# Starting the attention head pairs before the low-rank projections are done, and alternating the kinds of pair

## The reference, cut to what matters

```python
a_q, a_k, a_v, b_q, b_k, b_v, c_q, c_kv, c_kr = jnp.split(h @ w_in, IN_OFFSETS, axis=-1)
y_a = _window_attn(q_a, k_a, v_a, k_a_ctx, v_a_ctx, sink_a)      # 4 heads, windowed, with a sink
y_b = _gqa_core(q_b, k_b_all, v_b_all)                           # 4 heads, rms-normed q and k
q = _heads(_rms_norm(c_q, mla_q_norm) @ w_uq, C_HEADS)           # 8 heads, compressed path
k_nope, v = _rms_norm(c_kv, mla_kv_norm) @ w_uk, ... @ w_uv
y = concat(y_a, y_b, y_c) @ w_out
```

## Time and profile before

| what | value |
|---|---|
| median of 3 runs | 1936.54 us (1934.94 to 1938.43) |
| the profiled execution | 1939.29 us, its span 1937.5 us |
| granted clock, mean of the span | 0.953 |
| PE busy | 1744.1 us, 90% |
| DVE busy | 942.6 us, 49% |
| ACT busy | 645.5 us, 33% |
| mix0, from the fifth `uq` to the first `w_out` matmul | 945.47 to 1083.09 us |
| mix1, the same stretch | 1599.25 to 1694.86 us |

### The profile page before, as it was taken

How to read it: one execution, slowest core, us unless ns; L and a number is a source line. 1 busy time by engine, 2 the same in 40 slices (tenths; PEclk the granted TensorE clock), 3 DMA queues, 4 the chain that set the end, 5 groups by cost and what they waited for, 6 DMA issues and landing times.

```text
span 1937.5 us, 22581 instructions
## 1 busy us (share of the span) xinstructions
PE 1744.1 (90%) x9106; PEld 1191.6 (61%) x9106; DVE 942.6 (49%) x1702; ACT 645.5 (33%) x1110; POOL 94.8 (5%) x136
## 2 busy tenths in 40 slices
PE   6988967998998779989989979999999798889998
PEld 5654733444676334447445658888888574578886
DVE  5573410002344000144487465888766756755555
ACT  2155121122232112132266445222222424655443
POOL 0790000000000000000000000000000100000000
PEclk8998989999999889999989989999999898999999
DMA  9977499999857999982200112445544131024540
GB/s 395 377 304 319 173 416 416 421 421 421 364 215 324 409 405 417 422 348 87 87 1 1 44 44 87 180 189 191 200 181 189 38 114 44 1 87 174 176 172 22
DMA packets 62899, 430.04 MB, mean 222 GB/s; under 512 B 6592, under 2 KB 10816, under 8 KB 10944
## 3 DMA queue, kind: packets, MB, share of 16 engines
q1 hardware_dynamic: 62784, 428.48, 55.4%
HBM read 427.40 MB, written 1.05 MB: 221 GB/s over the span
## 4 chain that ended last, share of the span: by engine, by line
PE 64%; DVE 15%; DMA 10%; ACT 7%; issue 2%; SPq 1%; DVEq 0%; ACTq 0%
PE bank L292 14%; PE bank L1100 12%; PE bank L296 8%; PE bank L298 8%; PE bank L297 8%; DMA ring<-in_ws_dram 7%; DMA work<-in_ws_dram 3%; DVE ring_halves L2457 3%; ACT work_halves L2451 2%; PE bank L331 2%; PE bank L2110 1%; PE bank L2087 1%; DVE work L438 1%; PE bank L2555 1%; PE bank L2481 1%
## 5 line engine op out<-in xcount | busy, mean ns | idle before, releaser
L296 PE MATMUL bank<-work_halves 128*128 128x512 f32 (+1 forms) x1088 | 397.7, 366 | 25.8 <-DVE HH_halves L2886 8.5
L298 PE MATMUL bank<-work_halves,ring_halves 128*128 128x512 f32 (+1 forms) x1088 | 388.0, 357 | 0.0
L297 PE MATMUL bank<-HH_halves,work_halves 128*128 128x512 f32 (+1 forms) x832 | 288.6, 347 | 0.0
L1100 PE MATMUL bank<-ring,work 128*32 128x512 f32 (+2 forms) x896 | 258.6, 658 | 20.2 <-DMA work<-in_ws_dram 11.0
L1100 PE MATMUL bank<-work 128*32 128x512 f32 (+2 forms) x640 | 222.7, 650 | 33.9 <-DMA ring<-in_ws_dram 32.0
L296 PEld LDWEIGHTS bank<-work_halves 128*128 128x128 f32 x1088 | 208.7, 192 | 62.7 <-DVE HH_halves L2886 14.0
L298 PEld LDWEIGHTS bank<-work_halves,ring_halves 128*128 128x128 f32 x1088 | 208.5, 192 | 28.8
L2457 DVE TENSOR_TENSOR ring_halves<-ring,work_halves 128x2048 fp32r<-128x2048 f32 x72 | 163.6, 2288 | 51.0 <-ACT work_halves L2451 51.0
L297 PEld LDWEIGHTS bank<-HH_halves,work_halves 128*128 128x128 f32 x832 | 160.7, 193 | 20.7 <-issue 2.2
L1378 DVE TENSOR_TENSOR work<-work,bank 128x512 f32<-128x512 f32 x14 | 9.6, 688 | 296.7 <-PE bank L1100 296.7
L2451 ACT ACTIVATE work_halves<-ring 128x2048 fp32r<-128x2048 f32 x72 | 136.0, 1906 | 29.7 <-PE bank L298 28.0
(11 more groups left out here) (367 smaller groups left out, 2523.4 us busy)
## 6 DMA issues: line engine op xcount, KB each, us to landing
ring<-in_ws_dram SPq DMA_DIRECT2D x287, 1024.0 KB, 10.2
work<-in_ws_dram SPq DMA_DIRECT2D x117, 1024.0 KB, 17.9
con<-in_con_dram SPq DMA_DIRECT2D x1, 1177.0 KB, 27.5
XX<-in_xT_dram SPq DMA_DIRECT2D x1, 1024.0 KB, 10.2
XX<-in_cT_dram SPq DMA_DIRECT2D x1, 1024.0 KB, 21.3
out_dram<-XX SPq DMA_DIRECT2D x1, 512.0 KB, 3.6
out_dram<-XX SPq DMA_DIRECT2D x2, 256.0 KB, 2.8
par<-in_par_dram SPq DMA_DIRECT2D x1, 338.0 KB, 3.1
```

Of the source, the lines that this page charges most:

```text
L296: pe.matmul(out, l[0], r[0], start=start, stop=False)
L297: pe.matmul(out, l[0], r[1], start=False, stop=False)
L298: return pe.matmul(out, l[1], r[0], start=False, stop=stop)
L1100: m = pe.matmul(b[c, :], left[:, k, c], ring_of(self.w[i])[:, 512 * k:512 * k + 512], start=first and k == 0, stop=last and k == 3, skip_g ...
```

## The change

The late steps are taken out of the first part but for `uq` 0 to 3. Their order becomes uq 4, uq 5, rot 0, uq 6, uq 7, rot 2, uk 0, uk 1, rot 4, uk 2, uk 3, rot 6, uk 4 to 7, uv 0 to 3, and they are dealt out over the first eight pairs, up to three to a pair (`share`), one behind each of PE's three pieces of work in an iteration. They use banks 6 and 7 in turn; meanwhile scores have 0, 1, 2 and results only 5. ACT and DVE get the matching copies: the first of an iteration ahead of ACT's part of `act_rest` and the exponentials (on DVE behind the maxima), the others at the iteration's end.

The pairs are listed by hand. In mix0 the first eight are the A and B pairs of the context queries, alternating (256 keys); then four times A 512, C 512, C 256 and four times B 512, C 512, C 256. In mix1 the first eight are A and B in turn, then the eight C.

The two splits of `w_out` move to iterations 19 and 21 (mix0) and 9 and 11 (mix1) on ACT, at the end of the iteration, and to the head of the next iteration on DVE. The score buffers `sc` now lie where the first split writes. After the square root for `kB`, ACT does one small Exp into an unused column.

```diff
-                for h in range(8):
+                for h in range(4):
                     ro.take("uq", h)
                     self.events.append(("uq", h))
...
+                rest = [("uq", 4), ("uq", 5), ("rot", 0), ("uq", 6), ("uq", 7), ("rot", 2), ("uk", 0), ("uk", 1), ("rot", 4), ("uk", 2), ("uk", 3), ("rot", 6)]
+                rest += [("uk", h) for h in range(4, 8)] + [("uv", i) for i in range(4)]
+                if self.last:
+                    pairs = [(0, 0), (0, 2), (0, 1), (0, 3), (1, 0), (1, 2), (1, 1), (1, 3)] + [(q, c) for q in range(2) for c in range(4, 8)]
+                    share = [3, 3, 3, 3, 2, 2, 2, 2]
+                else:
+                    pairs = [(2, 0), (2, 2), (2, 1), (2, 3), (3, 0), (3, 2), (3, 1), (3, 3)]
+                    share = [3, 3, 3, 3, 3, 3, 2, 0]
+                    for a in range(2):
+                        for i in range(4):
+                            pairs += [(i // 2, 2 * a + i % 2), (i // 2, 4 + 2 * a + i % 2), (2 + i // 2, 4 + 2 * a + i % 2)]
...
+                self.spare = len(share) + 1 if self.last else 19
...
+                    for u in self.pair(i):
+                        put(0, (0, 1, 2) if both else (0, 1, 2, 7), "s", u)
...
+                        for ev in self.between[i][j:j + 1]:
+                            put(3, (6, 7), *ev)
...
                 for i in range(len(self.units) // 2 + 2):
                     for u in self.pair(i):
                         self.pe_scores(pe, u)
+                    for ev in self.between[i][0:1]:
+                        self.pe_late(pe, ev)
                     for u in self.pair(i - 1):
                         self.pe_turn(pe, u)
+                    for ev in self.between[i][1:2]:
+                        self.pe_late(pe, ev)
                     if i >= 2:
                         self.pe_values(pe, 2 * i - 4)
+                    for ev in self.between[i][2:3]:
+                        self.pe_late(pe, ev)
...
+                        if name == "kB":
+                            act.activation(small[:, 250:251], ones[:, 0:1], ACT.Exp)
...
                 for i in range(len(self.units) // 2 + 1):
-                    if i in (3, 5):
-                        self.ffn.split_act(act, i // 4)
+                    for ev in self.between[i][0:1]:
+                        self.act_late(act, ev)
...
+                    for ev in self.between[i][1:3]:
+                        self.act_late(act, ev)
+                    if i == self.spare:
+                        st.wait_ge(act, "qrope", 6)
+                        self.ffn.split_act(act, 0)
+                    if i == self.spare + 2:
+                        self.ffn.split_act(act, 1)
...
-                    if i in (4, 6):
-                        self.ffn.split_dve(dve, i // 5)
+                    if i == self.spare + 1:
+                        self.ffn.split_dve(dve, 0)
+                    if i == self.spare + 3:
+                        self.ffn.split_dve(dve, 1)
                     for u in self.pair(i):
                         self.dve_most(dve, u)
+                    for ev in self.between[i][0:1]:
+                        self.dve_late(dve, ev)
```

More of the change, by code:

```diff
@@ L1817, in __init__ @@
                 self.buf2 = [work[:, WORK - CW * (i + 1):WORK - CW * i] for i in range(3)]
-                wk, at = area(self.base)
-                self.sc = [wk(516) for _ in range(2)]
+                self.sc = [work[:, WORK - CW + 516 * i:WORK - CW + 516 * i + 516] for i in range(2)]
+                wk, at = area(scratch)
                 self.pr = [wk(516) for _ in range(4)]
@@ L1863, in __init__ @@
                 assert not live
[L1864 to L1869, removed]
                 self.scratch = {}
@@ L1873, in __init__ @@
                         self.scratch[ev[1]] = len(self.scratch)
[L1874 to L1884, removed]
+                self.rots = [[work[:, WORK - 2 * CW + 1024 * i + 512 * j:WORK - 2 * CW + 1024 * i + 512 * j + 512] for j in range(2)] for i in range(2)]
@@ new lines, in __init__, with put @@
+                assert sum(share) == len(rest) and sorted(pairs) == [(q, c) for q in range(self.n // 128) for c in range(8)]
+                self.units = [(q, c, r) for q, c in pairs for r in range(2)]
+                self.spare = len(share) + 1 if self.last else 19
+                self.between = [[rest.pop(0) for _ in range(share[i])] if i < len(share) else [] for i in range(len(pairs) + 2)]
+                at = [0, 0, 0, 0]
+                def put(kind, banks, *key):
+                    ro.put(banks[at[kind] % len(banks)], *key)
+                    at[kind] += 1
@@ new lines, in __init__ @@
+                for i in range(len(pairs) + 2):
+                    both = i < len(share)
+                    for u in self.pair(i):
+                        put(0, (0, 1, 2) if both else (0, 1, 2, 7), "s", u)
+                    for j in range(3):
+                        if j == 1:
+                            for u in self.pair(i - 1):
+                                put(1, (3, 4), "t", u)
+                        if j == 2 and i >= 2:
+                            put(2, (5,) if both else (5, 6), "o", 2 * i - 4)
+                        for ev in self.between[i][j:j + 1]:
+                            put(3, (6, 7), *ev)
@@ L2083, in pe_turn @@
                 st = self.st
-                b = bank_of(pe, st, self.T, "t", u)
+                b = bank_of(pe, st, self.ro, "t", u)
                 st.wait_ge(pe, "p", u)
@@ L2209, in act_exp @@
                 else:
-                    act.activation(p[:, 0:n], bank[self.S.of["s", u][0]][:, 0:n], ACT.Exp, bias=nm, accum_out=den).then_inc(st.act("exp", u), 1)
+                    act.activation(p[:, 0:n], bank[self.ro.of["s", u][0]][:, 0:n], ACT.Exp, bias=nm, accum_out=den).then_inc(st.act("exp", u), 1)
                     st.at["evicted", ("s", u)] = st.at["exp", u]
@@ L2223, in scratch_free @@
                     st.wait_ge(eng, "scratch", name)
-                st.wait_ge(eng, "evicted", ("cq1", 0))
-                st.wait_ge(eng, "evicted", ("ckv", 0))
-                st.wait_ge(eng, "uq", 7)
-                st.wait_ge(eng, "uv", 3)
-                st.wait_ge(eng, "shared keys")
+                st.wait_ge(eng, "used", self.win[4])
             def dve_gains(self, dve):
```

142 lines of the change are left out of this document (72 added, 70 removed).

## The result

The changed kernel took 1918.11 us (median of 4, 1915.9 to 1924.51) against 1937.49 us before (median of 4): a ratio of 0.9907, 95% interval 0.9893 to 0.9922, so 19.4 us less. The same two kernels timed a second time gave 1919.95 against 1939.04, 0.9908 [0.9893 to 0.9922]. The executions of the changed kernel lie further apart (8.6 us) than those of before (4.6).

A forecast was written before the change was run, and what follows sets the result against it. PE and DVE waiting for each other in turn was taken as the bound; 13.0 us less in mix0 and 6.9 in mix1, with 1 us for the clock, made 18.9 less: 1917.6 us, range 1907 to 1929.

The forecast's parts named there:

- the layout's own case: Whole kernel: the hand-laid order's sum holds, 18.9 us less, own range 1910 to 1926, chance 0.64.
- the change-over: Between late steps and pairs in the old order: 12.2 us of rot, first maxima and Exp table load, PE partly half rate.
- (a): First eight pairs with late steps beside them: iteration 8 begins at 35.4 us in mix0, 46.8 in mix1.
- the slower rival: First eight pairs: late steps wait for banks 6 and 7 and delay divisions; 1941 at 1.5 us a slot, chance 0.09.
- (b): Pairs after the first eight: 78.8 us in mix0, 30.5 in mix1; alternation itself gives some 2.5 us.
- (c): The w_out splits: DVE waits about 2.3 us for ACT; 5.2 us lost a stage, 5.5 in mix0.
- (d): From the end of the last values to the first w_out matmul: 4.95 and 6.2 us, unchanged.
- (e): PE's clock in the new order's gaps: 1 us lost in all, gaps mostly like one that kept 2.4 GHz.
- The rival of the falling clock: First eight iterations and behind the splits: PE falls to 1.2 GHz, costing 8 to 12 us; 1928, chance 0.15.
- the rule on bursts: Skill page's claim on PE: bursts with waits fall to half rate repeatedly; interleaving would take 8 to 12 us more.
- The bounds: Limits set on the terms for both stretches: together 34 us less than before at one end, 2 more at the other.
- the rival in which PE stays fed: Both stretches: banks no hindrance, splits fall into DVE's slack; 28 us less, 1909, up to 34, chance 0.12.

The follow-up runs named there:

- mix0 alone: The changed kernel with mix1 put back to its old steps, pair order, buffers and split places, small Exp kept early: 1925.45 us, ratio 0.9946.
- The splits in halves: The changed kernel with each of DVE's two parts of the w_out splits cut into two of 1024 columns, ahead of four pairs in turn: 1910.83 us, 0.9861.
- the first step: The changed kernel with DVE's parts of the two w_out splits one pair later in both stages, ACT's unmoved: 1914.83 us, ratio 0.9873.
- filling: The changed kernel with scores of the pair behind each w_out split computed again into the same bank: 1918.25 us, ratio 0.9905.
- its change-over filled: The kernel before with the last rot done five times and pair 1's scores three times in both stages: 1942.09 us, ratio 1.0025.

## Why the prediction was right, and where it was not

**The whole.** 19.4 us less for 18.9 predicted, the layout's own case. The direction and the cause hold: the change-over is gone and the late steps lie beside pairs. But the two profiles of the changed kernel show 12.4 and 14.9 us in the stretches where it laid out 19.9. Mix0 took 134.4 and 131.9 us for 124.6, mix1 86.4 in both for 88.7: mix0 gave less than half of its 13.0 in these profiles (7.4 in the one with mix0 alone), mix1 more than its 6.9. The work between the stages gave 1.1 us in the first profile (516.16 to 515.02) and nothing in the second (516.48). The start of mix0, behind code that nobody touched, lay between 940.9 and 946.6 us in the profiles, so one profile against one can't settle the last 4 to 5 us. That the total hit so closely is in part luck, and where the rest of the measured gain lies stays open.

**(a) The first eight pairs with late steps.** 38.15 us for 35.4 in mix0, 45.28 for 46.8 in mix1. PE's busy time there was 35.26 for 33.8; its waits came to 2.9 us. The feared banks 6 and 7 made PE wait 2.3 us in mix0, for DVE's copies (1.52 the longest), and 2.3 in mix1, 1.30 of them for ACT's copy of a `uq` and the rest for DVE: far from the 15 us a stage at which the prediction would have failed, and the slower rival has no place here. The layout had 1.6 to 2.4 us in each of three iterations of mix1. The price of late work in mix1 was summed slightly low: the rows give 10.63 + 16 x 0.44 = 17.65 us, not 17.4.

**(b) The other pairs.** The twelve with A: 42.69 for 41.2. Alternation was called worth 2.5 us in mix0; by idle time it was 0.5 to 1.8 there (16.3 to 15.9, 14.6 or 14.5) and 2.6 in mix1, which the sum had not counted by itself, and by the medians 7 to 8 in all, for which the profiles don't account.

**(c) The splits** went as told, apart from the clock: DVE waited 1.0 and 2.0 us for ACT in the first profile and 1.0 and 1.1 in the second (2.3 predicted), and PE behind it, 2.24 and 3.26 us, together the 5.5 that I had for mix0 (4.4 in the second). From 1025.79 to the end of the last values in the steady order at 1074.14 it took 48.35 us for 43.1, 5.2 more, of which 4 is busy time at the lower clock. The splits in halves show what could be had there: 7 to 9 us.

**(d) The end** was 5.2 us for 4.95, in mix1 within the 41.13 for 41.9 of everything behind iteration 8.

**(e) The clock** is the term that failed: 1 us taken, 7.4 and 6.2 us of busy time measured in the two profiles, nearly all behind gaps of 1.3 to 3.3 us. I had read from the window at 1660 that such gaps leave the clock alone. The rival of the falling clock was thus partly true; set against it is that the old order had 12.2 us in the same way. Whether a gap is followed by a fall was not the same in each execution: behind the first split of mix0 the changed kernel kept 1.00 in one profile (gap 2.24 us) and went to 0.70 in the other (2.25). The Trainium skill, page "TensorE: Matmul & The Clock Gate", section "What's actually happening", says of a kernel's start that the number of matmuls at the lower level differs between runs of the same kernel; these traces show such a difference in the middle of one. Of the rule on bursts that the prediction named, half is borne out: falls behind gaps at the splits, none in mix0's first 20 iterations, where the windows of both profiles have 1.00.

**The bounds** were added up wrongly. The terms' own limits give 39 us less than before at one end and 6 more at the other, not 34 and 2, and the terms of the rival in which PE stays fed give more than its 28. The result lies far inside either way.

**The table load** was costed at nothing after the change, and rightly so: it ran at 936.27, beside a DVE reciprocal. Without the early Exp it costs 4 to 6 us where 2.6 were named, but the excess is not clear of noise.

## What to carry to other kernels

Take a piece of work that two engines hand to each other and leave a whole unit of other work between its two halves; if the waiting engine has little slack per unit, cut the piece to that slack. That gave 7 to 9 us here, the first step 5 to 7 of them. And when a stretch changes length, split it into idle time and busy time of the bound engine first: here a busy time that moved with the same instructions was the clock. Then test whether that time counts, since a clock that was kept up by filling gained next to nothing.

## What was not expected of the hardware

- In the kernel before with its change-over filled, PE fell from 2.4 to 1.2 GHz with no gap in its work: 4.00 us busy of 4, the granted clock 0.50 from 964 to 976 us, at first in matmuls of 32x32 weights, then in scores. In the kernel before, half as many of the 32x32 matmuls (3.62 us) ran at 1.00.
- A gap of 1.30 us on PE in mix1 was followed by some 3.4 us at 0.50 in both profiles of the changed kernel and by none in the profile with the halves, whose order in that stage is the same up to there; gaps of 2.24 and 3.26 us in one execution, only the second with a fall.
- A table load of 1.28 us that moved onto the path made mix1's stretch 2.3 us longer and mix0's 0.5 or 3.0, by which profile it is compared with.
